# Token numbers fetched beside column copies, first columns on three engines, 1 MB of gate weights loaded early, in a block of attention and experts

## What is computed

```python
h = rmsnorm(x, ffn_norm_g[l])
x = x + hierarchical_moe(h, ...)

def hierarchical_moe(h, rg_w, rg_b, re_w, re_b, w_gate, w_up, w_down):
    g_sel = jnp.argmax(g_logits, axis=-1)                      # group of the token
    top_v, top_i = lax.top_k(e_logits, TOP_K)                  # two experts in it
    gate = g_gate * jax.nn.softmax(top_v, axis=-1)
    ...
    def expert_block(args):
        xb, e = args
        return (jax.nn.silu(xb @ w_gate[e]) * (xb @ w_up[e])) @ w_down[e]
    ...
    out = jax.ops.segment_sum(ys, slot_tok, num_segments=T)
```

## Time and profile before

| | us |
|---|---|
| median of 3 runs | 1741.24 (1740.82 to 1741.37) |
| the profiled execution, whole | 1744.3 |
| its span, first to last instruction | 1742.5 |
| stages before the first expert block | about 700 |
| expert blocks | about 1042 |

### The profile page before, as it was taken

How to read it: one execution, slowest core, us unless ns; L and a number is a source line. 1 busy time by engine, 2 the same in 40 slices (tenths; PEclk the granted TensorE clock), 3 DMA queues, 4 the chain that set the end, 5 groups by cost and what they waited for, 6 DMA issues and landing times.

```text
span 1742.5 us, 25966 instructions
## 1 busy us (share of the span) xinstructions
PE 1530.3 (88%) x7008; PEld 868.5 (50%) x7008; DVE 601.1 (34%) x726; ACT 365.7 (21%) x705; POOL 450.8 (26%) x2198
## 2 busy tenths in 40 slices
PE   7999999999999998887977977977977977987977
PEld 7787777588885666232332332332332332332323
DVE  6655666632234335021221221221321231221214
ACT  6422334522222443201001001010010110010101
POOL 4560073400000000332232233233233233233230
PEclk9999999999999999998988988988999998998989
DMA  8433222542222114899999999999999998999984
GB/s 291 112 82 96 81 65 73 195 102 97 97 97 97 49 49 197 335 429 395 409 375 379 415 374 375 411 379 377 406 380 379 411 378 357 412 376 375 411 337 194
DMA packets 88922, 472.66 MB, mean 271 GB/s; under 512 B 5026, under 2 KB 43084, under 8 KB 62924
## 3 DMA queue, kind: packets, MB, share of 16 engines
q1 hardware_dynamic: 87800, 470.84, 67.8%
q0 software_dynamic: 880, 0.35, 0.4%
q10 hardware_dynamic: 100, 0.03, 0.0%
HBM read 466.99 MB, written 4.21 MB: 270 GB/s over the span
## 4 chain that ended last, share of the span: by engine, by line
PE 36%; POOLq 22%; issue 18%; POOL 12%; DMA 6%; DVE 4%; ACT 2%; SPq 0%; DVEq 0%; ACTq 0%
POOLq L695 20%; POOL proj_buffer L700 12%; PE ps L1965 10%; PE ps L1839 9%; DMA proj_buffer<-block_ids 4%; PE ps L2018 3%; PE ps L2258 3%; POOLq L700 1%; DMA weight_ring<-in_xkv_w_dram 1%; PE ps L1801 1%; PE ps L2348 1%; PE ps L2081 1%; ACT weight_ring L889 1%; PE ps L1894 1%; PE ps L2217 1%
## 5 line engine op out<-in xcount | busy, mean ns | idle before, releaser
L2258 PE MATMUL ps<-weight_ring,proj_buffer 128*64 128x512 f32 x2032 | 480.8, 629 | 134.6 <-POOL proj_buffer L700 134.6
L700 POOL COPY proj_buffer<-transposed_acts 128x16 f32 x1984 | 300.9, 214 | 666.1 <-issue 607.4
L2258 PEld LDWEIGHTS ps<-weight_ring,proj_buffer 128*64 128x64 f32 x2032 | 181.5, 145 | 429.0 <-issue 405.8
L1647 DVE TENSOR_TENSOR residual<-ps,residual 128x1024 f32<-128x1024 f32 x128 | 150.8, 1220 | 346.4 <-PE ps L2217 345.6
L2284 PE MATMUL ps<-weight_ring,proj_buffer 128*64 128x512 f32 x960 | 214.2, 599 | 19.5 <-DVE proj_buffer L1657 18.5
L1663 DVE SCALAR_TENSOR_TENSOR y_low<-ps,proj_buffer,y_high 64x1024 fp32r<-64x1024 f32 x60 | 77.0, 1283 | 236.7 <-ACT y_high L1082 235.7
L2284 PEld LDWEIGHTS ps<-weight_ring,proj_buffer 128*64 128x64 f32 x960 | 68.0, 138 | 148.2 <-issue 145.2
L1071 ACT ACTIVATE proj_buffer<-ps 128x512 f32<-128x512 f32 x32 | 19.1, 598 | 531.3 <-PE ps L2258 531.3
L1082 ACT ACTIVATE y_high<-ps,proj_buffer 64x1024 fp32r<-64x1024 f32 x60 | 66.5, 1109 | 289.9 <-PE ps L2284 289.2
L1839 PE MATMUL ps<-mix_high,w_in_high 128*128 128x512 f32 x288 | 117.3, 407 | 1.3 <-issue 1.3
L1839 PE MATMUL ps<-mix_high,w_in_low 128*128 128x512 f32 x288 | 112.3, 390 | 0.0
(11 more groups left out here) (322 smaller groups left out, 1814.9 us busy)
## 6 DMA issues: line engine op xcount, KB each, us to landing
weight_ring<-in_expert_w_down_dram SPq DMA_DIRECT2D x63, 2048.0 KB, 12.1
weight_ring<-in_expert_w_gate_dram SPq DMA_DIRECT2D x62, 2048.0 KB, 10.3
weight_ring<-in_expert_w_up_dram SPq DMA_DIRECT2D x61, 2048.0 KB, 15.6
weight_ring<-in_w_in_dram SPq DMA_DIRECT2D x18, 1024.0 KB, 5.6
weight_ring<-in_w_out_dram SPq DMA_DIRECT2D x16, 1024.0 KB, 5.0
weight_ring<-in_xkv_w_dram SPq DMA_DIRECT2D x8, 1024.0 KB, 7.7
residual<-in_x_dram SPq DMA_DIRECT2D x8, 1024.0 KB, 12.9
weight_ring<-in_xq_w_dram SPq DMA_DIRECT2D x4, 1024.0 KB, 9.8
```

Of the source, the lines that this page charges most:

```text
L700: ins = g.tensor_copy(xsT[:, :, par * SLOTS + at + j], H[:, :, ds(where[j], 1)].rearrange("p k n -> p (k n)"))
L1647: v.tensor_tensor(part, ps[:, bank:bank + 2, :].rearrange("p b n -> p (b n)"), part, ALU.add).then_inc(signal, 1)
L2258: ins = mm(ps[side * SLOTS:(side + 1) * SLOTS, 0, :], xsT[:, k, par * SLOTS:(par + 1) * SLOTS], gate_up_weights(e, u, kk), start=(k == 0), ...
```

## The change

It does five things.

1. In the loop of POOL, the fetch of the next pair's token numbers (`load_ids(it + 1)`) is issued after the last 32 numbers of the current pair are in registers and ahead of their 32 copies. The wait for it stays at the head of the next pass. `ids_dram` has one more row, since the last pass fetches too.
2. Block 0's 64 columns are split 26 to ScalarE, 12 to VectorE, 26 to POOL; block 1's 28 to ScalarE, 36 to POOL. The store of all token numbers to DRAM moves between blocks 0 and 1 on POOL.
3. The first half (1 MB) of gate unit 0 of expert 1 is loaded to `second_gate`, in a part of proj_buffer, when the activations are transposed, ahead of `table_ready`. TensorE reads it there.
4. The first half of that place in the ring is thus free early, and takes the first half of gate unit 0 of expert 2 ahead of its turn; expert 2's loads are written out, the loop starts at 3.
5. `keep_busy(6)` becomes `keep_busy(20)`; `last_act_t` lies in another buffer.

```diff
-            for half in range(2):
-                for u in range(2):
-                    if half == 0:
-                        sp.wait_ge(first_used, u + 1)
-                    else:
-                        sp.wait_ge(used, UE + u + 1)
-                    sp.dma_start(unit(u)[:, half * CHK:(half + 1) * CHK], expert_unit(1, u)[:, half * CHK:(half + 1) * CHK]
-                                 ).then_inc(landed[unit_slot(u)], 16)
+            sp.wait_ge(first_used, 2)
+            load_half(1, 1, 0)
+            for u in range(2):
+                sp.wait_ge(used, UE + u + 1)
+                load_half(1, u, 1)
             load_units(1, 1, (2, 4, 5))
+            sp.dma_start(unit(0)[:, 0:CHK], expert_unit(2, 0)[:, 0:CHK]).then_inc(half_gate_in[1], 16)
+            sp.wait_ge(used, 2 * 6 + (UE - 6 + 1))
+            load_half(2, 0, 1)
+            load_units(2, 2, range(1, 6))
...
-            with sp.Fori(2, NE - 2) as b:
+            with sp.Fori(3, NE - 2) as b:
...
-                    if at == 0:
+                    if at == 0 and free is not None:
                         pool.wait_ge(gu_copied, free)
-                    for j in range(32):
+                    if at + n == SLOTS and loaded is not None:
+                        loaded()
+                    for j in range(n):
...
-            for par in range(2):
-                copy_columns(first_row[0:1, par * SLOTS:(par + 1) * SLOTS], par, 32, first_rows[par])
+            copy_columns(first_row[0:1, 0:SLOTS], 0, BY_ACT + BY_DVE, first_rows[0])
+            pool.wait_ge(ids_ready, 1)
+            pool.dma_start(ids_dram[0:NBLK // 2, :].rearrange("j (e s) -> (j e) s", e=2), ids[:, :]).then_inc(ids_stored, 16)
+            copy_columns(first_row[0:1, SLOTS:2 * SLOTS], 1, 28, first_rows[1])
...
             def pair_columns(it):
-                pool.dma_start(first_row[0:1, :], ids_dram[ds(it, 1), :]).then_inc(pair_ids_in, 16)
                 landed_ids = pool.to_reg(it * 16)
                 pool.wait_ge(pair_ids_in, landed_ids)
-                block_columns(it * 2, 0)
-                block_columns(it * 2 + 1, 1)
-
+                for par in range(2):
+                    copy_columns(first_row[0:1, par * SLOTS:(par + 1) * SLOTS], par, 0, block_rows,
+                                 free=pool.to_reg(it * 2 + par - 1), loaded=(lambda: load_ids(it + 1)) if par else None)
+
+            load_ids(1)
...
+            dve.wait_ge(h_turned, 56)
+            _, where = nc.values_load_multi_w_load_instructions(
+                first_row[0:1, BY_ACT:BY_ACT + BY_DVE], engines=(mybir.EngineType.DVE,), min_val=0, max_val=S - 1)
+            for j in range(BY_DVE):
+                ins = v.tensor_copy(xsT[:, :, BY_ACT + j], H[:, :, ds(where[j], 1)].rearrange("p k n -> p (k n)"))
+            ins.then_inc(first_rows[0], 1)
...
-            keep_busy(6)
+            keep_busy(20)
```

More of the change, by code:

```diff
@@ L177, in hybrid_block @@
         gu = PB[:, 8192:8192 + FF]
-        last_act_t = PB[:, 8704:8704 + KF * SLOTS]
+        last_act_t = Hf[:, 0:KF * SLOTS]
         scr = ring[:, NA * CHK:NSLOT * CHK]
@@ L509, in _ @@
                 sp.dma_start(unit(u), expert_unit(1 if u == 3 else 0, u)).then_inc(landed[unit_slot(u)], 16)
+            sp.wait_ge(h_turned, 56)
+            sp.dma_start(second_gate, expert_unit(1, 0)[:, 0:CHK]).then_inc(half_gate_in[0], 16)
             sp.wait_ge(table_ready, 1)
@@ L524, in load_expert, with load_half @@
                 load_units(e, b, range(6))
-            for half in range(2):
-                for u in range(2):
-                    if half == 0:
-                        sp.wait_ge(first_used, u + 1)
-                    else:
-                        sp.wait_ge(used, UE + u + 1)
-                    sp.dma_start(unit(u)[:, half * CHK:(half + 1) * CHK], expert_unit(1, u)[:, half * CHK:(half + 1) * CHK]
-                                 ).then_inc(landed[unit_slot(u)], 16)
+            def load_half(e, u, half):
+                part = slice(half * CHK, (half + 1) * CHK)
+                sp.dma_start(unit(u)[:, part], expert_unit(e, u)[:, part]).then_inc(landed[unit_slot(u)], 16)
+            sp.wait_ge(first_used, 2)
[3 more added lines that the diff above has]
+                load_half(1, u, 1)
             load_units(1, 1, (2, 4, 5))
+            sp.dma_start(unit(0)[:, 0:CHK], expert_unit(2, 0)[:, 0:CHK]).then_inc(half_gate_in[1], 16)
+            sp.wait_ge(used, 2 * 6 + (UE - 6 + 1))
+            load_half(2, 0, 1)
+            load_units(2, 2, range(1, 6))
             more = sp.value_load(meta[0:1, NOVER:NOVER + 1], min_val=0, max_val=NOVER)
-            with sp.Fori(2, NE - 2) as b:
+            with sp.Fori(3, NE - 2) as b:
                 load_expert(b, b)
@@ L689, in _, with copy_columns @@
             g.memset(L[:, :, :], NEG).then_inc(logits_padded, 1)
-            def copy_columns(tokens, par, first, done, free=None):
+            def copy_columns(tokens, par, first, done, free=None, loaded=None):
                 for at in range(first, SLOTS, 32):
+                    n = min(32, SLOTS - at)
                     _, where = nc.values_load_multi_w_load_instructions(
-                        tokens[:, at:at + 32], engines=(mybir.EngineType.Pool,), min_val=0, max_val=S - 1)
-                    if at == 0:
+                        tokens[:, at:at + n], engines=(mybir.EngineType.Pool,), min_val=0, max_val=S - 1)
+                    if at == 0 and free is not None:
                         pool.wait_ge(gu_copied, free)
-                    for j in range(32):
+                    if at + n == SLOTS and loaded is not None:
+                        loaded()
+                    for j in range(n):
                         ins = g.tensor_copy(xsT[:, :, par * SLOTS + at + j], H[:, :, ds(where[j], 1)].rearrange("p k n -> p (k n)"))
@@ L1091, in _ @@
             act.wait_ge(hT_ready, 56)
-            for par in range(2):
+            for par, n in enumerate((BY_ACT, 28)):
                 _, where = nc.values_load_multi_w_load_instructions(
-                    first_row[0:1, par * SLOTS:par * SLOTS + 32], engines=(mybir.EngineType.Activation,), min_val=0, max_val=S - 1)
-                for j in range(32):
+                    first_row[0:1, par * SLOTS:par * SLOTS + n], engines=(mybir.EngineType.Activation,), min_val=0, max_val=S - 1)
+                for j in range(n):
                     ins = a.activation(xsT[:, :, par * SLOTS + j], H[:, :, ds(where[j], 1)].rearrange("p k n -> p (k n)"), ACT.Copy)
@@ L2195, in expert_landed @@
                 s = unit_slot(u)
+                if isinstance(b, int) and b in (1, 2) and u == 0:
+                    pe.wait_ge(half_gate_in[b - 1], 16)
                 if isinstance(b, int) and b == 0 and u == 3:
@@ L2201, in expert_landed @@
                         loads -= 1
-                    if u < 2 and not (isinstance(b, int) and b < 1):
+                    if u == 1 and not (isinstance(b, int) and b < 1):
                         loads += 1
@@ L2206, in gate_up_weights @@
             def gate_up_weights(b, u, kk):
+                if isinstance(b, int) and b == 1 and u == 0 and kk < 4:
+                    return second_gate.rearrange("p (k n) -> p k n", n=FF)[:, kk, :]
                 if isinstance(b, int) and b == 0 and u == 3:
```

13 lines of the change are left out of this document (7 added, 6 removed).

## The result

The changed kernel takes 1701.7 us (median of 4 runs, 1700.0 to 1705.6) against 1741.3 us beside it (4 runs, 1740.8 to 1743.0). The ratio is 0.9774, 95% interval 0.9754 to 0.9794. The gain is 39.6 us, a little over half of the 73.6 us forecast, and the time lies above the forecast range. Beside the experiments further down, the kernel before took 1743.5 to 1744.3 us, and each ratio is taken against the runs beside it.

A forecast was written before the change was run, and what follows sets the result against it. POOL's chain was taken to bound at 65.03 us a pair, ahead of DMA at 59.0. Net 69.7 us from the hidden fetch plus 3.9 at the start gave 73.6 off 1741.24: 1667.6 us, range 1658 to 1682.

The forecast's parts named there:

- POOL bounds at 65.03 us a pair, and the landing can be hidden: POOL's expert loop: chain sets 65.03 us a pair; fetching under the last copies removes a 5.53 us wait, 14 times.
- POOL's period of 60.0 us: POOL's loop after the change: 65.03 - 5.53 + 0.48 = 60.0 us a pair, between 59.5 and 65.0.
- The start: Blocks 0 and 1: first fetch 3.9 us earlier, PE up to 1 us sooner, unit 3's load 6.5 us later.
- the 0.233 us a register: POOL's reading of token numbers: cost per register, used to size the shorter chunks of blocks 0 and 1.
- At 427 GB/s a pair takes 59.0 us, and a gain on POOL ends there: Weight stream: a pair's 25.2 MB at 427 GB/s takes 59.0 us, so a POOL gain ends there at the latest.
- that same window: Trace of the kernel before, 750 to 820 us: DMA share 1.01, engines moving 427 GB/s.
- The later share of 0.94: DMA share after 820 us; the gap was put where all six units have landed and PE is at their start.
- Rival A: Weight stream becomes the bound at 60.9 us a pair, giving 1678 us; chance 0.20.
- rival C: POOL's loop: a second 5.9 us instruction-fetch stall a pass, 1756 us, chance 0.04; no-change form, 1741, shares 0.04 with D.
- B: Between POOL's passes: the 4.91 us idle belongs to the fetch and moves with it, 1676 us; chance 0.09.
- D: POOL's last copies wait for the fetch's landing, so 5.53 us stays: 1738 us; chance 0.04 together with C's no-change form.
- its own test: POOL's fetches and PE's waits: forecast wrong if fetches are 61 us apart or more, or PE no longer waits for POOL.

The follow-up runs named there:

- where the stream was relieved: Changed kernel with the second down unit of experts 3 to 29 loaded only by half: 1663.4 us, ratio 0.9541.
- the kernel without bounds: POOL reads its 32 numbers without the two range instructions per number; done to the changed kernel, this took 1644.5 us, ratio 0.9423.

## Why the prediction was wrong

**POOL bounds at 65.03 us a pair, and the landing can be hidden:** right. No DMA stands in POOL's way between pairs any more, and the fetch stands 0.48 us ahead of the first copy (771.37, 771.85; 0.48 taken). POOL's period of 60.0 us was 59.5 while nothing held it up, and 59.3 to the end where the stream was relieved.

**The start:** it looks better than it was, by luck. The first fetch came at 716.00 (716.2), PE's block 0 at 701.09 (up to 1 us before 700.75 was forecast), the tables' loads 6.1 us later (6.5). But the stages ahead of the experts, which the change does not touch, were 1.7 us shorter in this execution, as the two down loads of expert 0 show, before first and then changed:

```profile
664.21 4.82 SPq L509 DMA_DIRECT2D weight_ring<-in_expert_w_down_dram  x2
```

```profile
662.49 4.82 SPq L512 DMA_DIRECT2D weight_ring<-in_expert_w_down_dram  x2
```

Counted from these, the first fetch is 2.4 us earlier instead of 3.9, PE's block 0 is 2.0 us later instead of up to 1 earlier, and the tables' loads are 7.9 us later instead of 6.5. The direction holds for POOL's chain, and the later tables cost nothing that shows in this kernel. The reading behind the 0.233 us a register was wrong as well: it is the price of the two range instructions, and the registers themselves come with the one read of 2.04 us. The sums hold, since the changed kernel has both.

**At 427 GB/s a pair takes 59.0 us, and a gain on POOL ends there:** this is the step that failed. 59.0 was taken from bytes moved in a window, and a consumer waits for landings. In the trace of before the first and last landing of that same window follow from these issues and times to landing:

```profile
734.72 0.34 SPq L521 DMA_DIRECT2D weight_ring<-in_expert_w_up_dram  x1
weight_ring<-in_expert_w_up_dram SPq DMA_DIRECT2D x1, 2048.0 KB, 13.6
...
799.59 0.33 SPq L521 DMA_DIRECT2D weight_ring<-in_expert_w_up_dram  x1
weight_ring<-in_expert_w_up_dram SPq DMA_DIRECT2D x1, 2048.0 KB, 20.1
```

From 748.32 to 819.69 us there are 14 steps in 71.37 us: 5.10 us each, 61.2 us a pair, where the bytes say 59.0. From 899.05 to 951.32, 10 steps, they are 5.23 us apart, 62.7 a pair. The long steps of 5.5 to 6.2 us were there to be seen. Bytes and landings differ as long as the engines ahead of the slow one have further loads to work on; a window at share 1.01 can be one in which they still have. The later share of 0.94 was put down to PE alone, but the changed kernel, with loads always waiting, still shows 95.9%. With the 62.9 that the changed kernel shows for 59.0, the same sum would have been 65.03 - 62.9 = 2.1 us a pair from block 4 on, 8.3 us won by then, and 8.3 + 13 x 2.1 = 36 us: 1705 us, against 1701.7 measured.

**Rival A** had the right mechanism, with a chance of 0.20, and was mis-sized by the same step: 60.9 us a pair, and 1678. Its signs came as told, PE waiting for weights with POOL waiting for its buffer. The 95 instruction packets of the earlier trace rows were read, but for their bytes (0.2% of the engines), and only as a stall of POOL in rival C. Neither their effect on the stream nor the possible gain from a shorter loop was seen.

**Rivals B, C and D:** none. B's 4.9 us did not move with the fetch: 8.90 us lie ahead of it, as much as reading 32 numbers and the 0.5 us of issue take, and 14.10 us between the last copies and the next pass's first (776.69 to 790.78) hold the branch. No chunk shows a new stall (C), and the copies start with the fetch's end (D). The forecast was wrong by its own test: fetches over 61 us apart and PE no longer waiting for POOL.

## What to carry to other kernels

Take a stream's floor from the times between landings of its loads over several periods, not from the bytes moved in a full window: the first is what consumers wait for, and here it was 4 us in 63 higher. A loop that an engine repeats beside a full weight stream should be short enough that its instructions are not fetched in every pass; look at the packets of the instruction queue by count and not by share. When one engine's chain is cut, look at the second bound with the same care, since the forecast ends there.

## What the runs showed that was not expected

- Instruction packets of 8.2 KB each cost a stream of 2 MB loads 0.63 to 0.69 us a packet, 0.31 for themselves and 0.35 in the packet of weights behind them. Their share of the DMA engines' time is 0.2%, what they cost is 4.1 us in 62.9, 6.5% of the stream's time.
- POOL's loop was fetched anew at about 522, 458 and 394 instructions (5 to 6.2 packets a pair) and not at 266 (2 packets in 780 us).
- Two waits written ahead of a column came out as one instruction a column: a loop's length is to be counted in the profile, not in the source.
- Of the time that POOL takes to read a number into a register, most is the two range instructions: with them a chunk of 32 took 13.2 us, without them 5.6 (1004.36 to 1009.97 in the kernel without bounds).
